# Three attentions of a two-block transformer: inverse roots formed on GpSimd, sliding keys turned a token tile sooner

## The reference, cut to what matters

```python
def rms_norm(x, gain):
    y = xf * lax.rsqrt(jnp.mean(xf * xf, axis=-1, keepdims=True) + EPS)
    return y * gain

def mla_attention(...):          # 8 heads of 96 = 64 + 32 rotary
    q = rms_norm(q, q_gain)      # per token and head
    k = rms_norm(k, k_gain)      # k = [k_nope, k_pe shared by the heads]
    ...
def nsa_attention(...):          # compressed, selected and sliding keys
    kw = partial_rope(rms_norm(k_w, kw_gain), cos, sin)   # the sliding keys
    ...
def differential_attention(...): # in each of the two layers, 4 heads of 64
    a = p[:, :, 0] - lam * p[:, :, 1]
    o = rms_norm(a @ v, g_head) * (1.0 - lam_init)
```

## Time and profile before

| what | us |
|---|---|
| median of 3 runs (2209.67 to 2212.11) | 2210.19 |
| the profiled execution | 2209.41 |
| its span | 2207.6 |
| TensorE busy in it | 2147.7 |
| VectorE, ScalarE, GpSimd busy | 1504.0, 954.0, 1195.1 |
| mean granted clock of TensorE | 0.996 |

### The profile page before, as it was taken

How to read it: one execution, slowest core, us unless ns; L and a number is a source line. 1 busy time by engine, 2 the same in 40 slices (tenths; PEclk the granted TensorE clock), 3 DMA queues, 4 the chain that set the end, 5 groups by cost and what they waited for, 6 DMA issues and landing times.

```text
span 2207.6 us, 33182 instructions
## 1 busy us (share of the span) xinstructions
PE 2147.7 (97%) x12377; PEld 1839.9 (83%) x12377; DVE 1504.0 (68%) x2242; ACT 954.0 (43%) x1905; POOL 1195.1 (54%) x594
## 2 busy tenths in 40 slices
PE   6999999999999999999999999999999999999997
PEld 4788888877899988897887898888897887889886
DVE  6834777554666692897746776677996727767676
ACT  3264663011556610644743555412545725555312
POOL 4747403776477677745016644577653037544675
PEclk9999999999999999999999999999999999999999
DMA  8422202522133333232002222322221012223221
GB/s 318 156 72 83 68 30 94 189 80 96 58 116 115 113 140 134 77 115 77 1 13 84 96 96 95 115 96 85 106 85 69 1 35 82 88 103 115 96 96 57
DMA packets 32776, 206.78 MB, mean 94 GB/s; under 512 B 4080, under 2 KB 4336, under 8 KB 11632
## 3 DMA queue, kind: packets, MB, share of 16 engines
q1 hardware_dynamic: 32192, 200.27, 25.2%
q10 hardware_dynamic: 432, 4.46, 0.5%
HBM read 202.61 MB, written 2.10 MB: 93 GB/s over the span
## 4 chain that ended last, share of the span: by engine, by line
PE 85%; DVE 8%; issue 2%; ACT 2%; DVEq 1%; DMA 1%; POOL 1%; POOLq 0%; SPq 0%; ACTq 0%
PE PS L1130 18%; PE PS L1132 18%; PE PS L1131 18%; PE PS L1626 4%; PE PS L1615 4%; PE PS L1385 3%; PE PS L1387 3%; PE PS L1386 3%; PE PS L1461 2%; PE PS L1463 2%; PE PS L1462 2%; PE PS L1640 2%; PE PS L1260 1%; PE PS L1263 1%; PE PS L1262 1%
## 5 line engine op out<-in xcount | busy, mean ns | idle before, releaser
L668 POOL TENSOR_TENSOR w_hi<-raw,zero_c 128x512 fp32r<-128x512 f32 (+1 forms) x135 | 281.6, 2104 | 545.0 <-PE PS L1132 543.7
L672 POOL TENSOR_TENSOR w_lo<-raw,w_hi 128x512 fp32r<-128x512 f32 (+1 forms) x135 | 365.0, 2722 | 5.8
L1130 PE MATMUL PS<-b_hi,w_hi 128*128 128x512 f32 x512 | 203.1, 397 | 1.0 <-POOL w_lo L891 1.0
L1132 PE MATMUL PS<-b_hi,w_lo 128*128 128x512 f32 x512 | 203.0, 396 | 0.0
L1131 PE MATMUL PS<-b_lo,w_hi 128*128 128x512 f32 x512 | 203.0, 396 | 0.0
L3376 DVE TENSOR_TENSOR b_lo<-a_all,b_hi 128x512 fp32r<-128x512 f32 x44 | 162.6, 3734 | 49.3 <-ACT b_hi L2511 49.3
L1130 PE MATMUL PS<-f_hi,w_hi 128*128 128x512 f32 x448 | 177.6, 396 | 0.7 <-DVE f_lo L2668 0.7
L1132 PE MATMUL PS<-f_hi,w_lo 128*128 128x512 f32 x448 | 177.6, 396 | 0.0
L1131 PE MATMUL PS<-f_lo,w_hi 128*128 128x512 f32 x448 | 177.6, 396 | 0.0
L691 POOL TENSOR_TENSOR w_lo<-raw,w_hi 128x512 fp32r<-128x512 f32 x48 | 71.1, 1481 | 92.7 <-ACT w_hi L2503 92.7
L1130 PEld LDWEIGHTS PS<-b_hi,w_hi 128*128 128x128 f32 x512 | 96.4, 188 | 24.7 <-POOL w_lo L891 1.2
(11 more groups left out here) (600 smaller groups left out, 6890.1 us busy)
## 6 DMA issues: line engine op xcount, KB each, us to landing
raw<-slabs_dram SPq DMA_DIRECT2D x161, 1024.0 KB, 4.8
aux<-ada_dram SPq DMA_DIRECT2D x18, 512.0 KB, 5.5
ada_first<-ada_dram SPq DMA_DIRECT2D x11, 512.0 KB, 14.2
cmpw<-cmpw_dram ACTq DMA_DIRECT2D x2, 2048.0 KB, 12.0
ada_late<-ada_dram SPq DMA_DIRECT2D x8, 512.0 KB, 3.4
ada_last<-ada_dram SPq DMA_DIRECT2D x8, 512.0 KB, 6.1
xT<-xT_dram SPq DMA_DIRECT2D x1, 2048.0 KB, 9.2
out_dram<-t SPq DMA_DIRECT2D x4, 512.0 KB, 3.2
```

Source lines behind the costliest of these rows:

```text
L668: high = nc.gpsimd.tensor_tensor(w_hi[:, slot, c], raw[:, slot, c], zero[:, 0:c.stop - c.start], ALU.add)
L672: low = nc.gpsimd.tensor_tensor(w_lo[:, slot, c], raw[:, slot, c], w_hi[:, slot, c].bitcast(f32), ALU.subtract)
L1130: nc.tensor.matmul(out, a_hi_, b_hi_, start=start, stop=False)
L1132: return nc.tensor.matmul(out, a_lo_, b_hi_, start=False, stop=stop)
```

## The change

GpSimd gets a function `inverse_root`: multiply by 1/d and add EPS, raise to the power -0.5 (with a column that a new `memset` fills at the start), and one Newton step, y (1.5 - 0.5 v y y), six instructions with a drain behind each. It is called ahead of the scaling of the MLA heads on 64 columns, as soon as `mla_sum` is there, and in each layer on 16 columns, behind the split of two slabs of the output projection, as soon as `diff_sum` is there. The roots on ScalarE and the reciprocals on VectorE in these three places are gone, with the semaphores `mla_root` and `mla_inv`. The sliding keys are turned after tile 0, and ScalarE writes their high parts ahead of the copy of tile 0. In `run` the loop is left out where it has no round.

```diff
@@ -410,6 +410,7 @@
         eps_c = small[:, 0:1]
         norm1_b = small[:, 48:56]
         lam_c = small[:, 2:3]
+        power_c = small[:, 46:47]
 
 
         const_loaded, crow_loaded, x_loaded = sem("const_loaded"), sem("crow_loaded"), sem("x_loaded")
@@ -453,7 +454,7 @@
         latents_inv = sem("latents_inv")
         q_taken_act, q_taken_dve = sem("q_taken_act"), sem("q_taken_dve")
         kv_done, kv_taken = sem("kv_done"), sem("kv_taken")
-        mla_sq, mla_sum, mla_root, mla_inv = sem("mla_sq"), sem("mla_sum"), sem("mla_root"), sem("mla_inv")
+        mla_sq, mla_sum = sem("mla_sq"), sem("mla_sum")
         mla_q_ready, mla_k_ready = sem("mla_q_ready"), sem("mla_k_ready")
         mla_turned, mla_act, mla_dve = sem("mla_turned"), sem("mla_act"), sem("mla_dve")
         attended, combined = sem("attended"), sem("combined")
@@ -650,6 +651,7 @@
 
         @block.gpsimd
         def _(pool):
+            nc.gpsimd.memset(power_c, -0.5)
             nc.gpsimd.memset(zero_c[:], 0.0).then_inc(zero_ready, 1)
             pool.wait_ge(zero_ready, 1)
             zero = zero_c[:, 0:1].to_broadcast([P, SLAB])
@@ -817,9 +819,25 @@
                 nc.gpsimd.tensor_tensor(x2, e, f, ALU.add)
                 pool.drain()
 
+            def inverse_root(v, d, y, e):
+
+                nc.gpsimd.tensor_scalar(v, v, 1.0 / d, EPS, ALU.mult, ALU.add)
+                pool.drain()
+                nc.gpsimd.tensor_tensor(y, v, power_c.to_broadcast(list(v.shape)), ALU.pow)
+                pool.drain()
+                nc.gpsimd.tensor_tensor(e, y, y, ALU.mult)
+                pool.drain()
+                nc.gpsimd.tensor_tensor(e, e, v, ALU.mult)
+                pool.drain()
+                nc.gpsimd.tensor_scalar(e, e, -0.5, 1.5, ALU.mult, ALU.add)
+                pool.drain()
+                nc.gpsimd.tensor_tensor(v, e, y, ALU.mult)
+                pool.drain()
+
             def mla_heads():
 
-                pool.wait_ge(mla_inv, 1)
+                pool.wait_ge(mla_sum, 3)
+                inverse_root(stats[:, 144:208], MLA_QK, stats[:, 0:64], stats[:, 64:128])
                 q = q_m[:].rearrange("p t (h d) -> p t h d", d=MLA_QK)
                 heads_by(q, stats[:, 144:176])
                 q_pe = q[:, :, :, MLA_NOPE:]
@@ -859,9 +877,10 @@
                 if n0 % 2:
                     split(1, n0, n0 // 2)
                     n0 += 1
-                with pool.Fori(n0 // 2, n1 // 2) as i:
-                    for s in (0, 1):
-                        split(s, 2 * i + s, i)
+                if n1 // 2 > n0 // 2:
+                    with pool.Fori(n0 // 2, n1 // 2) as i:
+                        for s in (0, 1):
+                            split(s, 2 * i + s, i)
                 if n1 % 2:
                     split(0, n1 - 1, n1 // 2)
 
@@ -869,6 +888,14 @@
             at = 2 * n_pieces + 2
             for n in [mlp0] + [mlp0 + N_UP + N_DOWN + layer * PER_LAYER + first for layer in range(LAYERS)
                                for first in (0, N_IN2 + N_WOUT)]:
+                for layer, ct in enumerate(COUNTS):
+                    if n == ct.up:
+                        for k in (at, at + 1):
+                            split(k % 2, k, k // 2)
+                        at += 2
+                        pool.wait_ge(diff_sum, layer + 1)
+                        inverse_root(stats[:, 0:16], HD, stats[:, 16:32], stats[:, 32:48])
+                        pool.drain().then_inc(diff_root, 1)
                 run(at, n)
                 at = n + 2
                 for k in (n, n + 1):
@@ -1060,7 +1087,7 @@
                                 O2[:, :, 64 * h:64 * h + 64], strip2[:]))
 
         DILATED_AT = 48
-        DIFF_SQ, DIFF_SUM, DIFF_ROOT, DIFF_SCALE = 58, 60, 62, 64
+        DIFF_SQ, DIFF_SUM, DIFF_SCALE = 58, 60, 64
         O2_TURNS = [(56, 4, 3), (59, 5, 7), (63, 0, 10), (67, 6, 8), (70, 7, 8), (73, 1, 12), (80, 2, 14)]
         o2_step = {step: n for n, (step, _, _) in enumerate(O2_TURNS)}
 
@@ -1829,7 +1856,7 @@
                                      wh[:, k, 512 * hf:512 * hf + 512], wl[:, k, 512 * hf:512 * hf + 512],
                                      k == 0, k == 1)
                 last.then_inc(kv_done if tt < TT - 1 else slab_used, 1)
-                if tt == 1:
+                if tt == 0:
                     pe.wait_ge(kw_ready, 1)
                     pe.wait_ge(q_taken_dve, 1)
                     nsa_turn(REP + 1, 3)
@@ -2298,10 +2325,10 @@
 
             act.wait_ge(c_summed, 1)
             q_squares(0)
+            keys_high(1, 3)
             take_kv(0)
             act.wait_ge(q_taken_dve, 2)
             q_squares(1)
-            keys_high(1, 3)
             for tt in (1, 2, 3):
                 take_kv(tt)
             act.drain()
@@ -2314,10 +2341,6 @@
                         A(pe_sq[:], z_tail[:, :, TAIL_PE:TAIL], ACT.Square)
                     A(m_sq[half][:, 0:2 * MLA_HEADS * MLA_NOPE].rearrange("p (t h d) -> p t h d", t=2, d=MLA_NOPE),
                       kv_x[:, 2 * half:2 * half + 2, :, 0:MLA_NOPE], ACT.Square).then_inc(mla_sq, 1)
-                if step == 8:
-                    act.wait_ge(mla_sum, 3)
-                    A(stats[:, 144:208], stats[:, 144:208], ACT.Sqrt, scale=1.0 / MLA_QK, bias=eps_c
-                      ).then_inc(mla_root, 1)
                 if step - 1 in mla_step and mla_step[step - 1] % 2 == 0:
                     n = mla_step[step - 1]
                     act.wait_ge(mla_turned, n + 1)
@@ -2616,9 +2639,6 @@
                     if step == DIFF_SQ:
                         act.wait_ge(out_used, m0 + 8)
                         A(sq_2[:], O2[:, :, 768:1024], ACT.Square).then_inc(diff_sq, 1)
-                    if step == DIFF_ROOT:
-                        act.wait_ge(diff_sum, layer + 1)
-                        A(stats[:, 0:16], stats[:, 0:16], ACT.Sqrt, scale=1.0 / HD, bias=eps_c).then_inc(diff_root, 1)
 
                 def single_turns(step):
                     if step - 1 in turn_step:
@@ -3160,9 +3180,6 @@
                     sk = stats[:, 176:208].rearrange("p (t h) -> p t h", t=TT)
                     V.tensor_tensor(sk, sk, stats[:, 208:212].unsqueeze(2).to_broadcast([P, TT, MLA_HEADS]), ALU.add
                                     ).then_inc(mla_sum, 1)
-                if step == 10:
-                    dve.wait_ge(mla_root, 1)
-                    V.reciprocal(stats[:, 144:208], stats[:, 144:208]).then_inc(mla_inv, 1)
                 if step - 1 in mla_step and mla_step[step - 1] % 2:
                     n = mla_step[step - 1]
                     dve.wait_ge(mla_turned, n + 1)
@@ -3554,7 +3571,6 @@
                                         axis=AX.X).then_inc(diff_sum, 1)
                     if step == DIFF_SCALE:
                         dve.wait_ge(diff_root, layer + 1)
-                        then(V.reciprocal(stats[:, 0:16], stats[:, 0:16]))
                         then(V.tensor_scalar(stats[:, 0:16], stats[:, 0:16], 1.0 - LAM_INIT[layer], None, ALU.mult))
                         scale_heads(O2[:, :, 768:1024].rearrange("p t (h d) -> p t h d", d=HD), stats[:, 0:16],
                                     row("diff", layer * HD, HD))
```

## The result

The change makes the kernel slower. In 12 runs each, the changed kernel took 2214.18 us (median; 2211.86 to 2217.24) and the kernel before 2211.10 (2208.20 to 2213.63). The ratio is 1.0017, with a 95% interval of 1.0010 to 1.0025, so the change costs 2.2 to 5.5 us. The forecast was 2202.3, in a range of 2200.0 to 2207.0, and faster.

The account below looks back on a forecast made before the run. TensorE, busy 97% of the span, was taken as the bound; 1.47 + 6.1 - 0.3 + 0.65 = 7.9 us off 2209.41 gave 2201.5, and 0.8 more for the median 2202.3, range 2200.0 to 2207.0.

Parts of the forecast that it names:

- their geometric middle, 1.1 us: GpSimd's power on the MLA heads' 64 columns, taken between 0.32 and 3.8 us; gives a stall of 0.3 us.
- the upper bound of 3.8: Highest price for the 64-column power: thirty plain passes at 1.87 ns a column, 3.6 us, 3.8 with overhead.
- GpSimd becomes the bound, slower: Rival, chance 0.12: a power above 8.9 us for 64 columns eats the gain; at 16 us, 2221.0 us.
- the keys decide: MLA heads: GpSimd does the queries' half first, the keys' last, so the keys set TensorE's stall, 0.3 us.
- The turn: Sliding keys turned after tile 0: TensorE's gap ahead of tile 3 goes entirely, 1.47 us won.
- The square root of the MLA heads: First attention: root and table loads leave ScalarE; 6.1 us won, 2.84 in gaps and 3.25 from half clock.
- The layers: Differential heads' root in both layers: VectorE's reciprocal goes, 0.32 us each, 0.65 together, if GpSimd is in time.
- The clock falls anyway: Rival, chance 0.18: gaps gone, but the low clock comes elsewhere in the attention; gain 5.0 us, 2205.2.
- A dear first call: Within the dear-power rival (0.12; power 3.8 to 8.9 us, 2207.2 at 6): first call costs about 6 us.

Follow-up runs that it names:

- e1: The kernel before with only the sliding keys turned after tile 0 and their high parts ahead of tile 0's copy; 2209.09 us against 2211.60, ratio 0.9992.
- e2: The changed kernel with a plain product in place of the power, so the inverse roots are not formed; 2202.85 us, ratio 0.9956.
- e4: The kernel before with the root on GpSimd in the two layers only, turn and MLA root as before; 2210.64 us, ratio 0.9998.
- e8: e5 with the power written in place and no Newton step, in all three attentions; 2203.85 us against 2210.75, ratio 0.9963.
- e3: The changed kernel with the queries' 32-column power ahead of the keys' and the second slab's split behind the heads; 2212.78 us, ratio 1.0005.
- e6: e3 with the second slab's split cut into four pieces of 512 columns, at the same place; measured once, 2205.95 us.
- e5: e3 with the second slab's split waiting until the last group of MLA heads is turned; 2206.07 us against 2210.75, ratio 0.9978.
- e7: The changed kernel with the MLA heads' 64-column power done a second time into the same place; measured once, 2223.15 us.
- e10: e5 with VectorE's scaling in the layers one step later, step 65 in place of 64; 2204.15 us against 2210.89, ratio 0.9969.

## Why the prediction was wrong

**The step that failed is one term: "I take their geometric middle, 1.1 us", for the power.** It measured 10.55 us, beyond the upper bound of 3.8 too. That bound rested on thirty plain passes, a number that no row gave; the measured power is 10.55 / 0.32 = 33 of the plain instructions, but some 88 of the passes of 1.87 ns that the bound was counted in (165 ns a column). A middle between two ends twelve times apart, of which one is guessed, is no estimate; and the sum hung on it, since the stall by the forecast's own terms, 2.44 + power - 3.26, left the power 0.82 us of cover.

**The rival came true, at its own point.** "GpSimd becomes the bound, slower", with a chance of 0.12, was to decide above 8.9 us, or 139 ns a column. Its formula, 8.2 - (10.55 - 0.82), gives 1.5 us slower, and 2.6 with 0.5 for each layer by its own rule. The medians say 3.1. Its stall is 9.7 us, all of it waiting. TensorE's waits are 6.8, and it loses 11.4; what the rival left out is the clock behind the two waits. It also said that the keys decide; the queries were late as well, and each had its own wait and its own low stretch.

**The turn: right.** 1.47 forecast; 1.7 in the table for the changed kernel, 1.6 in e1.

**The square root of the MLA heads: right in sum, half right in kind.** 6.1 forecast; the changed kernel wins 6.2 between 215 and 235. But e1 shows that the low clock can stay away with the gaps still there, and that the 3.3 us this wins are lost again by 259. And the cadence of the earlier trace rows, from which 6.1 was read, held a third part that was not seen. In the kernel before, the timeline of VectorE has the same 128x4 product:

```profile
233.58 1.16 DVE L2907 TENSOR_TENSOR stats<-stats,z_tail 128x4 f32<-128x4 f32 x1
239.49 0.42 DVE L2907 TENSOR_TENSOR stats<-stats,z_tail 128x4 f32<-128x4 f32 x1
244.00 0.17 DVE L2907 TENSOR_TENSOR stats<-stats,z_tail 128x4 f32<-128x4 f32 x1
```

Two heads were held for 0.99 and 0.25 us by GpSimd's scaling, 1.24 of the 15.0 us. Of these the change removes nothing, it moves them: in the changed kernel the product is held at 235.05, 244.65 and 255.83, for 2.5 us in sum. In e2, which has no power, the 6.2 us won by 235 are 5.2 at 259.

**The layers: wrong, and small.** 0.32 a layer forecast, on the condition that GpSimd is done in time. It was given 4.5 us for the root and took 4.7 (1110.40 to 1115.11), with 2.91 for the power of 16 columns, and VectorE waited 0.35: the reciprocal's time, given back. e4 measured nothing. Where the root is in time the term holds: in the table e2 wins 0.3 us in each layer, e8 0.3 and 0.4.

**The clock falls anyway: not as put.** From 200 to 245 it stays at 1.00. It falls behind new waits instead.

**A dear first call.** The Trainium skill ("GPSIMD Engine Reference", section "2.1 Instruction dispatch") gives a load of about 6 us with the first call of a freshly loaded kernel. No run here shows one for the power: e3's first power takes 5.44 us and its second 5.43, and none has more than 0.15 us of idle ahead of it.

## What to carry to other kernels

Ask of each new operation whether the trace holds one row with that operation on that engine; if none does, the price is unknown by an order of magnitude, and the forecast is the size of the cover against it, not a middle value. Work moved to an idle engine must be started when its input is ready, not when its whole batch is: half the columns early, with the split out of VectorE's way, turned a loss of 3 us into a gain of 5 to 7. And work on an idle GpSimd is not free for VectorE: put its long products where VectorE has no instruction with both operands in SBUF, or cut them short.

## What the runs showed of the hardware

**The power on GpSimd** takes 2.91, 5.44 and 10.55 us for 16, 32 and 64 columns of 128 partitions: about 0.16 us a column ((10.55 - 5.44) / 32) and 0.3 to 0.4 us beside. A product of 64 columns takes 0.32.

**VectorE is held by whole products of GpSimd.** A VectorE product with two operands in SBUF that starts beside one of GpSimd's plain products, sums or differences of two tiles ends with it: in the changed kernel 235.05 + 1.23 = 236.28 against the second of the four L801 (233.37 + 2 x 1.44 = 236.25); in e3 and e6 the three cases above. In the twelve traces the 128x4 product takes more than 0.2 us 44 times, and each time it ends 0.02 to 0.03 us after such an instruction of GpSimd. The reciprocal (0.17 to 0.18 us beside GpSimd's split in e6) and the products that read PSUM are not held. Once, in e6, it was by the lengths GpSimd that waited. The Trainium skill ("SBUF — State Buffer", section "Who interferes with whom") says that a VectorE instruction with two SBUF inputs and a GpSimd instruction that reads SBUF take turns on a shared pair of ports, each for a whole instruction; these rows agree. They don't for the power, which reads SBUF too: while it ran, from 220.90 to 231.45, the 128x4 product passed three times unhindered in the changed kernel's timeline of VectorE, and was held when the scaling came. In all the traces it met a power 15 times, and took 0.16 or 0.17 us each time.

```profile
222.25 0.17 DVE L2927 TENSOR_TENSOR stats<-stats,z_tail 128x4 f32<-128x4 f32 x1
226.50 0.17 DVE L2927 TENSOR_TENSOR stats<-stats,z_tail 128x4 f32<-128x4 f32 x1
230.80 0.16 DVE L2927 TENSOR_TENSOR stats<-stats,z_tail 128x4 f32<-128x4 f32 x1
235.05 1.23 DVE L2927 TENSOR_TENSOR stats<-stats,z_tail 128x4 f32<-128x4 f32 x1
```

**Left open.** Why gaps of the same length are followed by a low clock in one profile and not in another: 1.44 and 1.37 us in e1 (1.00 behind them), 1.47 and 1.37 in the earlier trace rows (0.52), 1.45 and 1.37 in e4 (0.81). In the second layer the gaps do differ: e3, e5 and e6, where the clock fell, have one of 1.80 or 1.81 us, the changed kernel, e4 and e7, where it stayed at 1.00, one of 1.49, and e10 one of 1.54. In those three GpSimd stood 0.45 to 0.46 us ahead of one of the short instructions of the root; what it waited for there the traces don't show, nor does any run show that the 0.3 us more are what brought the clock down.
